# The feed-forward layer of a float32 kernel computed by Strassen's scheme: seven quarter products for eight

## What is computed

```python
mixed = concatenate([o, pooled], -1) @ w_out                     # 1024 x 1024 (output projection)
x = layer_norm(DN_ALPHA * x + mixed, ln1_g, ln1_b)
h = square(relu(x @ w_up)) @ w_down                              # 1024 x 4096, 4096 x 1024
x = layer_norm(DN_ALPHA * x + h, ln2_g, ln2_b)
ple = (p @ w_ple) * sigmoid(x @ w_ple_gate)
x = layer_norm(DN_ALPHA * x + ple, ln3_g, ln3_b)
```

## Time and profile before

| | |
|---|---|
| median of 3 runs | 4164.97 us |
| lowest, highest | 4164.79, 4167.02 us |
| the profiled execution | 4164.67 us |
| its span in the trace | 4162.9 us |
| mean granted TensorE clock | 0.983 of full |
| the layer in the trace | about 3287 to 4008 us |

### The profile page before, as it was taken

The page is one execution under the profiler, slowest core; times in us unless marked ns, Lnnn a source line. Parts: engine busy times, 40 slices in busy tenths (PEclk is TensorE's granted clock), DMA queues, the critical chain, the costliest instruction groups (busy, mean ns, idle before and its releaser), DMA issues.

```text
span 4162.9 us, 59315 instructions
## 1 busy us (share of the span) xinstructions
PE 3959.1 (95%) x26210; PEld 3198.6 (77%) x26210; DVE 1739.9 (42%) x2696; ACT 1324.5 (32%) x2213; POOL 1197.7 (29%) x613
## 2 busy tenths in 40 slices
PE   8899999999999999899999889999999999999997
PEld 4757676665998897677687777897888988888877
DVE  2545454533340258762215463332187432332344
ACT  3232323232332243562212353212275312212133
POOL 1202010102114356761232102343102523332354
PEclk9999999999999999999999999999999999999999
DMA  3101010003111121010011100130100211111111
GB/s 91 32 2 32 2 32 3 17 11 108 42 41 41 51 71 51 26 31 31 28 54 42 40 1 23 49 107 28 51 1 21 72 61 51 47 45 51 51 41 41
DMA packets 164977, 168.68 MB, mean 41 GB/s; under 512 B 8176, under 2 KB 152432, under 8 KB 164720
## 3 DMA queue, kind: packets, MB, share of 16 engines
q1 hardware_dynamic: 164720, 164.89, 12.5%
HBM read 156.48 MB, written 8.39 MB: 40 GB/s over the span
## 4 chain that ended last, share of the span: by engine, by line
PE 80%; DVE 9%; ACT 5%; POOL 4%; issue 2%; DMA 0%; POOLq 0%; DVEq 0%; ACTq 0%; SPq 0%
PE pair L641 16%; PE pair L643 16%; PE pair L642 16%; PE pair L606 10%; PE pair L629 3%; PE pair L617 2%; PE pair L1137 1%; PE pair L596 1%; PE pair L1327 1%; PE pair L791 1%; POOL H L3472 1%; PE pair L1297 1%; ACT BIG L2084 1%; PE pair L783 1%; POOL W_r L3414 1%
## 5 line engine op out<-in xcount | busy, mean ns | idle before, releaser
L641 PE MATMUL pair<-XT_r,W_r 128*128 128x512 f32 x1744 | 693.8, 398 | 8.5 <-ACT BIG L2022 1.9
L642 PE MATMUL pair<-BIG_r,W_r 128*128 128x512 f32 x1624 | 632.2, 389 | 0.0
L3414 POOL TENSOR_TENSOR W_r<-W,W_r 128x2048 fp32r<-128x2048 f32 (+1 forms) x74 | 327.1, 4420 | 741.2 <-ACT W_r L1475 741.2
L643 PE MATMUL pair<-XT_r,W_r 128*128 128x512 f32 x1232 | 480.1, 390 | 0.0
L641 PE MATMUL pair<-W_r,BIG_r 128*128 128x256 f32 (+1 forms) x1280 | 417.9, 326 | 1.5 <-DVE MIX_r L2774 0.4
L606 PE MATMUL pair<-XT,W 128*128 128x512 f32 x928 | 405.5, 595 | 3.2 <-POOL MIX L3287 2.2
L641 PEld LDWEIGHTS pair<-XT_r,W_r 128*128 128x128 f32 x1744 | 327.4, 188 | 85.3 <-issue 10.6
L643 PE MATMUL pair<-W_r,BIG_r 128*128 128x256 f32 (+1 forms) x1152 | 380.3, 330 | 0.0
L642 PEld LDWEIGHTS pair<-BIG_r,W_r 128*128 128x128 f32 x1624 | 305.0, 188 | 68.9 <-issue 6.7
L606 PEld LDWEIGHTS pair<-XT,W 128*128 128x128 f32 x928 | 175.1, 191 | 220.1 <-issue 218.6
L643 PE MATMUL pair<-W_r,MIX_r 128*128 128x256 f32 x960 | 271.6, 283 | 0.0
(11 more groups left out here) (440 smaller groups left out, 7744.3 us busy)
## 6 DMA issues: line engine op xcount, KB each, us to landing
W<-w_in SPq DMA_DIRECT2D x29, 1024.0 KB, 5.5
W<-w_in_e SPq DMA_DIRECT2D x33, 512.0 KB, 6.6
MIX<-w_up SPq DMA_DIRECT2D x15, 1024.0 KB, 5.3
MIX<-w_down SPq DMA_DIRECT2D x15, 1024.0 KB, 4.9
W<-w_in_o SPq DMA_DIRECT2D x12, 1024.0 KB, 5.0
W<-w_in SPq DMA_DIRECT2D x17, 512.0 KB, 4.1
H<-x SPq DMA_DIRECT2D x16, 512.0 KB, 9.2
W<-w_out SPq DMA_DIRECT2D x7, 1024.0 KB, 5.3
```

The source lines that it names most:

```text
L641: E.matmul(b[:, 0:n], lh, rh, start=k == ks[0], stop=False)
L642: E.matmul(b[:, 0:n], lh, rl, start=False, stop=False)
L643: mm = E.matmul(b[:, 0:n], ll, rh, start=False, stop=k == ks[-1])
L3414: G.tensor_tensor(WLO[k % 2][:, 0:n], WSTAGE[k % 2][:, 0:n], WHI[k % 2][:, 0:n], ALU.subtract).then_inc(*s_split.mark("split", k))
```

## The change

The layer is computed in eight units: up and down in turn, for four groups of 1024 hidden features. A unit is a product of 1024x1024 by 1024x1024, cut into four quarters of 512x512 on each side, and computed by seven products of 512x512 by 512x512 in place of eight (the form of Strassen's scheme with 15 additions). The products come in the order p1, p2, p6, p5, p7, p3, p4; g counts them over all units, 0 to 55. A product has four pieces k of 128 inner features, and each piece four banks i of 128 rows: 4 x 4 x 3 matmuls of 128x512. Even g use banks 4 to 7, odd g 0 to 3; p6, p7, p3 and p4 add to what the bank holds, and each product's banks are read: into HID (ScalarE for p1, p6, p5, p4, VectorE for p2, p7, p3, with relu and square) for up, into H (VectorE) for down.

The sums of operand quarters are made on GpSimd (weights, in place, in four slots of raw quarters) and on VectorE (x or HID, in SUM_1 and SUM_2 or in place). Each product's operands are split anew, ScalarE the high parts, GpSimd the low parts of the weights, VectorE those of x: `operand(side, k)` is one place for each piece k, so that piece k of product g + 1 is made when TensorE has left piece k of g. XT is kept in float32 (`split=False`). The weights come in pieces of 256 KB, 16 for a unit and 4 more, for the quarter that its sums have overwritten.

The output projection's last quarters use banks 4 to 7 (`for_last`), the normalisation before the layer banks 0 to 3 (`for_ln`); TensorE waits for the read of output (1, 0) before them. The first product (g = 0) stands where the first two up banks stood. The fillers named for these two are not issued any more; those at the tiles' transposes are. At the end, tiles 0 to 3 begin their normalisation during the last product and tiles 4 to 7 at the four embedding groups.

```diff
+        ORDER = (1, 2, 6, 5, 7, 3, 4)
+        UNITS = 2 * FF // D
+        LAST_P = 7 * UNITS - 1
+        QUAD = {1: (0, 0), 2: (0, 0), 6: (0, 1), 5: (1, 1), 7: (1, 1), 3: (0, 1), 4: (1, 0)}
+        def operand(side, k):
+            at = (4096, 6144, 0, 2048)[k] + 1024 * (side == "x")
+            return W_R[:, at:at + HALF], W_R[:, at + HALF:at + 2 * HALF]
...
         def pe_outp():
...
+                pe.wait_ge(*done("ev", "outp", "out", 1, 0))
                 for t in range(NT):
                     pe_out3(2, t)
                     pe_out3(3, t)
                     yield t
                 yield None
-                for ct in range(2):
-                    pe_up(0, 0, ct, done("ev", "outp", "tr", 3, 0), done("ev", "outp", "tr", 3, 1))
+                for k in range(4):
+                    pe_part(0, k)
                     yield None
+        def pe_part(g, k):
+            u, p = product_of(g)
+            left, right = (operand(side, k) for side in (("w", "x") if is_up(u) else ("x", "w")))
+            pe.wait_ge(*done("mlp", "lw", g, k))
+            pe.wait_ge(*done("mlp", "lx", g, k))
+            for i in range(4):
+                b, rows = sum_bank(g, i), slice(i * P, (i + 1) * P)
+                if k == 0:
+                    if g == 0:
+                        pe.wait_ge(*done("ev", "outp", "out", 3, NT - 1))
...
+                    else:
+                        pe.wait_ge(*done("mlp", "read", g - 2, i))
+                E.matmul(b[:, :], left[0][:, rows], right[0], start=k == 0 and p in (1, 2, 5), stop=False,
+                         skip_group_check=True)
+                E.matmul(b[:, :], left[0][:, rows], right[1], start=False, stop=False, skip_group_check=True)
+                mm = E.matmul(b[:, :], left[1][:, rows], right[0], start=False, stop=k == 3,
+                              skip_group_check=True)
...
         def act_mlp():
...
+                for g in range(1, LAST_P + 1):
+                    for k in range(4):
+                        act_snapshot(g - 1, k)
+                        if g < LAST_P:
+                            act_high_w(g + 1, k)
+                            act_high_x(g + 1, k)
+                        elif k == 1:
+                            act_split_high(gate, 0, done("gate", "staged", 0), done("mlp", "used", LAST_P, 0))
+                        yield k if g == LAST_P else None
                 for j in range(4):
                     for at in EMBED[3 * j:3 * j + 3]:
                         act_copy_out(gate, every, ("p", *at), HELD[at], HALF)
...
-                    yield None
+                    yield 4 + j
                 for k in range(2, G_EARLY):
                     act_gate_root(k)
                     yield None
...
+        def dve_low(g, k):
+            u, p = product_of(g)
+            high, low = operand("x", k)
+            dve.wait_ge(*done("mlp", "hx", g, k))
+            V.tensor_tensor(low, x_part(u, p, k), high, ALU.subtract).then_inc(*ff.dve.mark("mlp", "lx", g, k))
+        def dve_read(g, i):
...
+                if p in SNAPSHOT:
+                    dve.wait_ge(*done("mlp", "product", g, i))
+                    dve.wait_ge(*done("mlp", "read", number(u, SNAPSHOT[p]), i))
+                    V.tensor_tensor(h, h, b, ALU.add).then_inc(*ff.dve.mark("mlp", "read", g, i))
+                    dve.wait_ge(*ff.dve.last())
+                    V.scalar_tensor_tensor(h, h, 0.0, h, ALU.max, ALU.mult).then_inc(*ff.dve.mark("mlp", "hid", u, r, c, i))
+                elif p == 4:
+                    dve.wait_ge(*done("mlp", "read", g, i))
+                    V.tensor_tensor(h, h, h, ALU.mult).then_inc(*ff.dve.mark("mlp", "hid", u, r, c, i))
+                return
...
         def dve_mlp():
...
+                for g in range(1, LAST_P + 1):
+                    u, p = product_of(g)
+                    for k in range(4):
+                        dve_read(g - 1, k)
+                        if u == 0 and p == 2:
+                            dve.wait_ge(*done("ev", "outp", "tr", NT - 1, 0))
+                            dve_sum(0, 5, k)
+                            dve_sum(0, 6, k)
+                        if is_up(u) and p == 6:
+                            dve_sum(u, 4, k)
+                        if not is_up(u):
+                            for other in {1: (5, 6), 2: (7,), 6: (3,)}.get(p, ()):
+                                dve_sum(u, other, k)
+                            if u + 1 < UNITS and p in (7, 3):
+                                dve_sum(u + 1, 5 if p == 7 else 6, k)
+                        if g < LAST_P:
+                            dve_low(g + 1, k)
+                        if is_up(u) and p == 6:
+                            dve_sum(u, 7, k)
+                        yield k if g == LAST_P else None
...
         def pool_ln(st):
...
+                if st is outp and t == NT - 1:
+                    for k in range(2, 4):
+                        pool_low_w(0, k)
...
+        def pool_low_w(g, k):
+            u, p = product_of(g)
+            high, low = operand("w", k)
+            pool.wait_ge(*done("mlp", "hw", g, k))
+            G.tensor_tensor(low, w_part(u, p, k), high, ALU.subtract).then_inc(*ff.pool.mark("mlp", "lw", g, k))
...
         def pool_mlp():
+            for g in range(LAST_P):
+                u, p = product_of(g)
+                for k in range(4):
+                    pool_low_w(g + 1, k)
+                    if p == 1:
+                        for other in (5, 7, 6) if u == 0 else (6,):
+                            pool_sum(u, other, k)
+                    if p == 2:
+                        pool_sum(u, 3 if is_up(u) else 4, k)
+                    if p == 4:
+                        for other in (5, 7):
+                            pool_sum(u + 1, other, k)
...
         def sp_gate():
             for quarter in range(4):
-                sp.wait_ge(*(done("mlp", "split", 2 * FF // Q - 2 + quarter) if quarter < 2 else
+                sp.wait_ge(*(done("mlp", "lw", LAST_P, 3) if quarter < 2 else
```

More of the change, by code:

```diff
@@ L568, in out_ring, with ln_ring @@
         def out_ring(quarter, t):
-            return for_early if quarter < 2 and t >= 4 else every
+            if quarter >= 2:
+                return for_last
+            return for_early if t >= 4 else every
+        def ln_ring(st):
+            return for_ln if st is outp else every
         STAGE = [MIX_AREA[:, 2048 * i:2048 * (i + 1)] for i in range(2)]
         XL_M = BIG_R[:, 0:8192].rearrange("p (c n) -> p c n", c=KD)
-        HH, HL = (BIG_R[:, 8192 + 2048 * i:8192 + 2048 * (i + 1)].rearrange("p (c n) -> p c n", c=2) for i in range(2))
+        ORDER = (1, 2, 6, 5, 7, 3, 4)
@@ L1399, in steps @@
+                for g in range(1, LAST_P + 1):
+                    for k in range(4):
+                        pe_part(g, k)
+                        yield k if g == LAST_P else None
+                while len(every.order) % 8 != 4:
+                    every.open("mlp", "unused", len(every.order))
+                for b in (4, 5, 6, 7, 0, 1, 2, 3):
+                    every.open("mlp", "bank", b)
                 for j in range(4):
@@ L2230, in act_outp @@
             act_high(OUT3 + 2)
-            act_split_high(ff, 0, done("mlp", "staged", 0), done("chunk_free", OUT3 + 1))
-            act_split_high(ff, 1, done("mlp", "staged", 1))
+            act.wait_ge(*done("chunk_free", OUT3 + 1))
+            for k in range(2):
+                act_high_w(0, k)
             def steps():
@@ L2236, in steps @@
                 yield None
-                for ct in range(2):
-                    act_relu(0, 0, ct)
-                    yield None
-            follow(steps(), act_split_ln_tile(outp))
-        def act_relu(n, half, ct):
-            act.wait_ge(*done("mlp", "up", n, half, ct))
-            if n:
-                act.wait_ge(*done("mlp", "inner", n - 1, half, ct))
-            S.activation(RELU[2 * half + ct], every.bank("mlp", "up", n, half, ct)[:, :], ACT.Relu).then_inc(
-                *ff.act.mark("ev", "mlp", "up", n, half, ct))
+                act.wait_ge(*done("outp", "out", 3, NT - 1))
@@ L3217, in dve_mlp @@
+                for i in range(4):
+                    dve_read(LAST_P, i)
+                for i in range(4):
+                    yield 4 + i
             follow(steps(), dve_split_ln_tile(ff))
@@ new lines, in pool_sum @@
+        def pool_sum(u, p, k):
+            r0, r1, r2, r3 = (raw(u, role, k) for role in range(4))
+            dst, x, y = ({5: (r3, r2, r3), 7: (r2, r0, r2), 6: (r0, r3, r0), 3: (r1, r1, r0)} if is_up(u) else
+                         {5: (r0, r2, r0), 7: (r2, r3, r2), 6: (r3, r3, r0), 4: (r1, r1, r3)})[p]
+            for role in (0, 2, 3):
+                pool.wait_ge(*done("mlp", "raw", u, role, k))
+            pool.wait_ge(*ff.pool.last())
+            G.tensor_tensor(dst, x, y, ALU.add if is_up(u) and p == 5 else ALU.subtract).then_inc(
+                *ff.pool.mark("mlp", "w_sum", u, p, k))
```

(15 more changed lines are left out.)

270 lines of the change are left out of this document (156 added, 114 removed).

## The result

The changed kernel takes 4236.5 us (median of 4 runs, 4232.96 to 4241.88); the kernel before, run beside it, 4164.88. The ratio is 1.0172, with a 95% interval of 1.0154 to 1.019. The change is slower by 72 us.

What follows compares the result with a forecast made beforehand. TensorE was the bound before; VectorE and GpSimd meeting would set heavy stretches after. Layer 0.7 + 609.3 + 28 + 7.7 + 80 + 27, 32.1 later, tail +15.4, clock 4: +51.5 on 4164.67, forecast 4216 us, range 4138 to 4260.

Steps and rivals of the forecast that it cites:

- TensorE's saving: Feed-forward layer: 2688 matmuls, 384 fewer, take 609.3 us; alone that is -87 us.
- The round of 1.74: When VectorE's two-SBUF-input operations and GpSimd's operations are both queued, each engine does one in 1.74 us.
- Stretch A: p4 (up), p1, p2, p6 (down): ends at 63.5 us for TensorE's 43.5, loss 20, four times, +80.
- Stretch B: p4 (down), p1, p2, p6, p5 (up): ends at 63.4 us against 54.4, loss 9, three times, +27.
- Front: Start of the layer: first piece at R + 15, last R + 27, p6 starts about R + 50: +28 us.
- First unit's p6 and p5: These two products alone behave like Stretch B: 29.5 us for 21.8, +7.7.
- Clock: New TensorE waits may bring some matmuls at 1.2 GHz: 0 to 50 us, taken as 4.
- Tail: After the last product: tile 7's transposes done at 56.1 us, 50.3 to compare with 34.9 before, +15.4.
- GpSimd's 4.8 us for a tile: In the normalisation after the last product, GpSimd was taken to need 4.8 us for each tile.
- Edits at nothing: 160 DMAs of 256 KB, bank changes every three matmuls and four output banks for eight were taken to cost nothing.
- the first: Rival: TensorE keeps the bound because buffers swallow the meetings; R + 646, 4105 us, faster; chance 0.10.
- The second: Rival: VectorE and GpSimd bound, perfectly packed, 162.7 us for each pair of units; 4140 us, faster; chance 0.12.

Runs made afterwards that it cites:

- e0_again: The changed kernel run once more, with no edit, as the control: 4235.8 us.
- e1: Changed kernel with each of GpSimd's low parts and sums of the weights replaced by two fills that read nothing from SBUF: 4103.0 us.
- e7: Changed kernel with each of GpSimd's low parts and sums of the weights replaced by three fills of the same place: 4182.7 us.
- e3: Changed kernel with relu and square of HID moved from VectorE to ScalarE as two activations: 4196.4 us.
- e2: Changed kernel with the same operations, but one GpSimd weight sum and VectorE's sums moved from the fullest steps to others: 4187.4 us.
- e4: Changed kernel with ScalarE's first four sigmoids placed behind the scaling of tile 7: 4230.6 us.
- e5: Changed kernel with the edits of e2, e3 and e4 together: 4153.0 us.
- e8: e5 with the previous product's four banks read in the first two of a product's four steps: 4160.4 us.
- e9: e8 with three of a unit's four weight sums moved from GpSimd to VectorE from the second unit on, and HID sums made earlier: 4130.6 us.
- e6: e5 with all four weight sums of a unit moved from GpSimd to VectorE from the second unit on: 4172.3 us.
- e10: Changed kernel with only the previous product's four banks read in the first two of a product's four steps: 4214.3 us.

## Why the prediction was right, and where it was off

The forecast was 4216 (4138 to 4260), slower; measured 4236.5. The accounts are best made with e0_again's trace, whose R is that of before: span 4232.5 - 4162.9 = 69.6, of which the layer is 768.7 - 720.6 = 48.1 and all behind it 21.5. The forecast had 36.1 (clock included) and 15.4, 51.5 in all.

- **TensorE's saving**: right. 2688 matmuls at 0.227, 609.3, and e1 shows a layer of 633.6 where only these and the front are left.
- **The round of 1.74**: right, 1.70 measured, and the cause (e1, e7). It was read from two places of the old trace. Not every operation has a whole round: in a pair of the middle 70 of VectorE's 104 two-input operations took over 1 us.
- **Stretch A** (p4 to p6): 63.5 by queues; 10.9 + 14.5 + 20.0 + 17.9 = 63.3 measured. The waits stand where they were put: p2's first piece for ScalarE's read, 5.74, p6's for VectorE's.
- **Stretch B** (p4 to p5): 63.4 by queues; 10.9 + 12.7 + 11.9 + 13.3 + 18.0 = 66.8. The term "loss 9" was 12.4, three times: 10 us. The queue for p5's wait was worked with VectorE's additions free beside GpSimd; the waits for its third and fourth bank came to 1.2 and 3.7 us, and p5 was partly run at the half clock.
- **Front**: p6 of the first unit was put at R + 50 and started at 3346.99, R + 51.7 (e0_again 51.0). Inside it the first piece came at R + 10.6 for 15, the last at R + 27.3 for 27.
- **First unit's p6 and p5**: put at 29.5, measured 13.6 + 19.3 = 32.9 (e0_again 13.6 + 21.2 = 34.8). These 5 us, B's 10 and the front's 1 make 16; less the 4 taken for the clock, that is the 12 by which the layer was put too short.
- **Clock**: the step "I take 4" named the right effect and the wrong size. Matmuls lost 35.8 us at half clock. Most of that fell, as the text said, where others set the pace: A came out at 63.3 with it. The pair of units took 184.9 for 181.3, some 3.5 more each, in B; what of that is clock and what queue, no run separates. Nor does the clock's cost follow the sum of the waits: e3 has 7 us fewer waits than e2 and 13 us more at half clock.
- **Tail**: tile 7's transposes at 58.1 for 56.1. The larger part of the 6 us missed is a step that I had credited wholly: two gate products that now come earlier should give 5.8 back behind tile 7, and gave 1.6 (span end: 120.4 us after the transposes before, 118.8 in e0_again). TensorE waits 1.5 us there for tile 7's copy, and the clock behind a wait of 5.52 is low (0.77; the kernel before has 1.00 in the 16.5 us behind its transposes of tile 7):

```profile
4111.80 1.94 PE L698 MATMUL pair<-ident,H 128*128 128x128 f32 x8 [5.52 <-POOL H L3620]
4115.24 0.55 PE L710 MATMUL pair<-W_r,XT_r 128*128 128x256 f32 x1 [1.50 <-DVE BIG_r L2591]
```

```profile
4113.70:4130.00 16.30, 14.80 (x102) 14.79 (x102) 7.72 (x16) 2.06 (x6) 2.43 (x1) 0.77 0.55 180
```

- **GpSimd's 4.8 us for a tile**, in the same term, was too short: it holds for one of the first four tiles, the other three took 6.2 (4072.00, 4078.18, 4084.33, 4090.49), as in e4. Tiles 5, 6 and 7 were put at 36, 43 and 50 and started on GpSimd at 38.1, 44.7 and 51.3.
- **Sum**: 12 us short in the layer, 6 in the tail. The first profile's other 8 us stood ahead of R and did not return in e0_again: they belong to that execution.
- **Edits at nothing** (DMAs, bank changes, four banks for the outputs): e1 carries all of them and has 10.9 us for a product.
- **Rivals**: the first is what e1 shows, in which the two engines do not meet (layer 633.6 for 646, 4103 for 4105 us); in the changed kernel the round of 1.7 excluded it. The second had 162.7 for a pair, and the written order was 22 us above it. e5 and e8 came near it (165.6 and 167.2), but that it is a bound is not shown: by the 1.15 and 0.55 us of a turn, the 88 and 88 operations of e5 make 150 us, less than TensorE's 152.3, and the 64 and 112 of e9 make 135 where a pair took 159.9. What a pair takes beyond these sums is put down to the order of the queues against the due times; no run shows that by itself.

## What to carry to other kernels

When work leaves TensorE for VectorE and GpSimd, don't add up each engine's busy share: count the instructions of VectorE with two SBUF inputs and those of GpSimd that read SBUF, give the pair a round of both for each that meet (here 1.15 + 0.55 us), and compare that with TensorE's time, stretch by stretch between the due times; the mean load says too little. Moving operations out of the fullest stretches (e2) and to ScalarE (e3) each won 10 to 12 us in a pair. Moving work to the engine that holds the other for a shorter time, here VectorE, may pay even if it is the busier one, but only with an order that keeps VectorE's reads of PSUM banks in time: with the late reads of e6 it lost, with those of e9 it won. Reading the banks ahead of the operands won 29 us of the layer alone (e10) and nothing on top of e5 (e8).

## What the runs showed that I had not expected

- GpSimd's fills (527 ns for 128x512) leave VectorE's two-input operations at 692 ns; GpSimd's differences stretch them to 1304.
- A VectorE instruction of one element a lane with two SBUF inputs took 2.17 us, and 4.32 us behind a 128x2048 operation of GpSimd (changed kernel, 4061.58 to 4065.90, where GpSimd's operation ends at 4065.88): in both its duration was the rest of what GpSimd had in hand.
- A stop of TensorE of 5.74 us was followed by matmuls at 0.42 us. Over the changed kernel's layer, stops of 112.0 us brought 35.8 us of half clock, in e1 10.0 brought 3.8, in e9 39.6 brought 9.9.
